# Fourteen condition blocks of the later layers formed on VectorE inside the dense feed-forward stage

## What is computed

```python
cond = jax.nn.silu(c)                                   # 1 x 1024
for i in range(2):
    mod = cond @ ada_w[i] + ada_b[i]                    # 1024 x 6144 weights for each layer
    sh1, sc1, g1, sh2, sc2, g2 = jnp.split(mod, 6)
    h = rms_norm(x, norm_mix[i]) * (1.0 + sc1) + sh1
    y = mla_mixer(h, ...) if i == 0 else gdn_mixer(h, ...)
    x = x + g1 * y
    h = rms_norm(x, norm_ffn[i]) * (1.0 + sc2) + sh2
    y = swiglu_ffn(h, ...) if i == 0 else moe_ffn(h, ...)   # dense: 1024 -> 2816 -> 1024; moe: 8 experts
    x = x + g2 * y
```

## Time and profile before

| | |
|---|---|
| median of 3 runs | 2355.04 us (2353.94 to 2355.44) |
| the profiled execution's own time | 2351.56 us |
| its span | 2349.7 us |
| TensorE matmul busy | 2132.0 us, 91% of the span |
| VectorE busy | 730.6 us, 31% |
| ScalarE busy | 429.3 us, 18% |
| mean granted TensorE clock | 0.937 of 2.4 GHz |
| HBM read | 509.11 MB, 217 GB/s over the span |

### The profile page before, as it was taken

How to read it: one execution, slowest core, us unless ns; L and a number is a source line. 1 busy time by engine, 2 the same in 40 slices (tenths; PEclk the granted TensorE clock), 3 DMA queues, 4 the chain that set the end, 5 groups by cost and what they waited for, 6 DMA issues and landing times.

```text
span 2349.7 us, 32266 instructions
## 1 busy us (share of the span) xinstructions
PE 2132.0 (91%) x13962; PEld 1463.8 (62%) x13962; DVE 730.6 (31%) x1547; ACT 429.3 (18%) x899; POOL 38.1 (2%) x34
## 2 busy tenths in 40 slices
PE   7999885478999999999899999999998899999997
PEld 4554664477754444444575688886677778648844
DVE  3484278747321111111235210004573330001001
ACT  2210324122211111111233310003222120000001
POOL 1000111000000000000000000000000000000000
PEclk9999976689989999999998999999998879999999
DMA  9643000002579999999745834308410267899695
GB/s 313 230 144 107 1 1 1 2 2 75 216 296 428 424 428 427 429 428 429 278 154 176 286 126 171 124 27 298 168 73 2 72 249 251 319 392 351 248 345 227
DMA packets 161767, 511.98 MB, mean 218 GB/s; under 512 B 8926, under 2 KB 32173, under 8 KB 148973
## 3 DMA queue, kind: packets, MB, share of 16 engines
q1 hardware_dynamic: 160816, 509.87, 56.6%
q10 hardware_dynamic: 829, 0.31, 0.1%
HBM read 509.11 MB, written 1.05 MB: 217 GB/s over the span
## 4 chain that ended last, share of the span: by engine, by line
PE 83%; DVE 9%; DMA 3%; ACT 3%; issue 2%; POOL 0%; SPq 0%; ACTq 0%; DVEq 0%; POOLq 0%
PE PS L378 34%; PE PS L2206 9%; PE PS L2227 5%; PE PS L2360 4%; PE PS L2122 4%; PE PS L2133 3%; PE PS L2058 3%; PE PS L580 3%; PE PS L2311 2%; DMA work<-in_moe_w_gate_up_dram 2%; PE PS L588 2%; PE PS L737 1%; PE PS L729 1%; DVE sq L1648 1%; DVE work L1645 1%
## 5 line engine op out<-in xcount | busy, mean ns | idle before, releaser
L378 PE MATMUL PS<-hT,work 128*128 128x256 f32 x1456 | 327.2, 386 | 2.8 <-issue 2.4
L378 PEld LDWEIGHTS PS<-hT,work 128*128 128x128 f32 x1456 | 279.0, 193 | 45.6 <-issue 5.5
L378 PE MATMUL PS<-work 128*128 128x256 f32 (+4 forms) x960 | 284.9, 457 | 2.4 <-DVE work L1803 1.5
L378 PEld LDWEIGHTS PS<-work 128*128 128x128 f32 (+2 forms) x960 | 178.0, 187 | 103.9 <-issue 76.9
L2206 PE MATMUL PS<-work,sq 128*64 128x512 f32 x1024 | 222.6, 592 | 1.3 <-ACT sq L2151 1.3
L2206 PEld LDWEIGHTS PS<-work,sq 128*64 128x64 f32 x1024 | 76.7, 137 | 143.8 <-issue 143.8
L378 PE MATMUL PS<-sq,work 128*128 128x128 f32 x1408 | 159.6, 277 | 4.9 <-DMA work<-in_moe_w_gate_up_dram 3.5
L378 PEld LDWEIGHTS PS<-sq,work 128*128 128x128 f32 x1408 | 159.3, 194 | 6.8 <-issue 6.8
L2227 PE MATMUL PS<-work 128*64 128x512 f32 x512 | 113.4, 595 | 9.9 <-issue 9.9
L2360 PE MATMUL PS<-work 128*64 128x512 f32 (+1 forms) x352 | 114.4, 593 | 1.9 <-ACT work L2390 1.9
L2188 DVE COPY work<-PS 128x1024 f32<-128x1024 f32 x22 | 26.9, 1225 | 230.2 <-PE PS L2227 117.0
(11 more groups left out here) (567 smaller groups left out, 2218.6 us busy)
## 6 DMA issues: line engine op xcount, KB each, us to landing
work<-in_ex_gate_dram SPq DMA_DIRECT2D x32, 2048.0 KB, 12.1
work<-in_ex_up_dram SPq DMA_DIRECT2D x32, 2048.0 KB, 15.2
work<-in_ex_down_dram SPq DMA_DIRECT2D x32, 2048.0 KB, 10.9
work<-in_moe_w_gate_up_dram SPq DMA_DIRECT2D x32, 2048.0 KB, 10.0
work<-in_ada_w_dram SPq DMA_DIRECT2D x24, 2048.0 KB, 9.0
work<-in_moe_w_down_dram SPq DMA_DIRECT2D x16, 2048.0 KB, 14.9
work<-in_w_ada_dram SPq DMA_DIRECT2D x12, 2048.0 KB, 8.9
work<-in_moe_w_gate_up_dram SPq DMA_DIRECT2D x16, 1536.0 KB, 13.4
```

Source lines behind the costliest of these rows:

```text
L378: ins = pe.matmul(outp, lhs, rhs, start=n == 0, stop=n == len(pairs) - 1, **kw)
```

## The change

Blocks 22 to 35 leave their places and are made in the feed-forward stage. The weights of a block are no longer multiplied on TensorE: VectorE forms the weighted sum over the eight 128-row pieces with one multiply and seven multiply-and-adds of 128x512 (`ada_sum_dve`), each waiting for the one before, and TensorE then sums over the partitions and turns the row with four one-column matmuls against ones (`ada_sum_pe`). VectorE starts a block behind tiles 1, 2, 4, 5, 6, 8, 9, 10, 12, 13, 15, 16, 17 and 19 of the 22; TensorE takes it up two tiles later, between the gate and up products. The results go to bank 7, so the tiles rotate over three banks. The 14 loads stand among the gate, up and down units of the stage, the one-turn loop around the stage is written out, and the gate and up units are used when their own tiles are complete, as before.

```diff
+    FFN_ADA = {g: n for n, g in enumerate((1, 2, 4, 5, 6, 8, 9, 10, 12, 13, 15, 16, 17, 19), N_ADA - 14)}
+    FFN_UNITS = []
+    for e in range(2):
+        for t0, n in ((0, 4), (4, 4), (8, 3)):
+            FFN_UNITS += [("gate", e, t0, n), ("up", e, t0, n)]
+            FFN_UNITS += [("ada", FFN_ADA[11 * e + t]) for t in range(t0, t0 + n) if 11 * e + t in FFN_ADA]
+        FFN_UNITS += [("down", e, t0, n) for t0, n in ((0, 4), (4, 4), (8, 3))]
...
-    for name, n in (("w_out", 2), ("ada_b", 4), ("moe1", 96), ("ada_c", 2), ("mla", 2), ("mla_q", 3), ("ada_d", 10),
-                    ("mla_out", 2), ("ada_e", 1), ("ffn", 18), ("ada_f", 1), ("gdn_kq", 4), ("ada_g", 4), ("gdn_vz", 4),
-                    ("gdn_out", 2), ("ada_h", 2), ("moe2", 72)):
+    for name, n in (("w_out", 2), ("ada_b", 4), ("moe1", 96), ("ada_c", 2), ("mla", 2), ("mla_q", 3), ("ada_d", 4),
+                    ("mla_out", 2), ("ffn", len(FFN_UNITS)), ("gdn_kq", 4), ("gdn_vz", 4), ("gdn_out", 2), ("moe2", 72)):
...
+        elif name == "ffn":
+            released_ffn(*FFN_UNITS[j])
...
+    def released_ffn(what, e, t0=0, n=0):
+
+        if what == "ada":
+            sp.wait_ge(S["ada_evac"], e + 1)
+        elif what == "down":
+            sp.wait_ge(S["weights_used"], downs_before["ffn"] + 3 * e + t0 // 4 + 1)
+        else:
+            sp.wait_ge(S["gate_up"], ex_tiles["ffn"] + 11 * e + t0 + n)
...
+    ADA_BANKS_OF.update({n: (None, 7) for n in FFN_ADA.values()})
...
+    def ada_sum_dve(n):
+
+        u = place["ada", n]
+        arrived(u, eng=dve)
+        dve.wait_ge(S["ada_cols"], n - 1)
+        w, row = unit(u, KT, 512), late_row[n % 2]
+        dv.link(dve.tensor_scalar(row, w[:, 0, :], cond[:, 0, 2:3], None, ALU.mult))
+        for k in range(1, KT):
+            ins = dve.scalar_tensor_tensor(out=row, in0=w[:, k, :], scalar=cond[:, k, 2:3], in1=row, op0=ALU.mult, op1=ALU.add)
+            if k < KT - 1:
+                dv.link(ins)
+        ins.then_inc(S["ada_evac"], 1)
...
+    def ada_sum_pe(n):
+
+        pe.wait_ge(S["params"], 1 + ada_group(n))
+        pe.wait_ge(S["ada_evac"], n + 1)
+        for m in range(4):
+            ins = pe.matmul(PS[:, ADA_BANKS_OF[n][1], m:m + 1], late_row[n % 2][:, m * P:(m + 1) * P], ones[:, 0:1],
+                            start=True, stop=True)
+        ins.then_inc(S["ada_cols"], 1)
 
...
+    def ffn_sp():
+        for j, x in enumerate(FFN_UNITS):
+            if x[0] == "ada":
+                ada_load(x[1])
+            else:
+                what, e, t0, n = x
+                load(U["ffn"] + j, ex_src("ffn", what, t0, n, e))
...
-                            if g - g0 >= 4:
-                                pe.wait_ge(S["hidden"], i * n_it + (ex_tiles[name] + g - 3))
+                            if g - g0 >= nb:
+                                pe.wait_ge(S["hidden"], i * n_it + (ex_tiles[name] + g - nb + 1))
                             for j, w in enumerate((unit(ug, KT, n * P), unit(uu, KT, n * P))):
                                 paced = 8 if name == "ffn" and g == 0 and j == 0 else None
-                                ins = product(PS[:, 4 + (g - g0) % 4, j * N:(j + 1) * N],
+                                ins = product(PS[:, 4 + (g - g0) % nb, j * N:(j + 1) * N],
                                               [(w[:, k, ptile(name, t, n)], hT[:, k, :]) for k in range(KT)], paced=paced)
                                 if j == 0 and owed:
                                     ins.then_inc(S["pair_moe1"], owed)
                                     owed = 0
                                 if j == 0 and t == 0:
                                     arrived(uu, i * rounds)
+                                if name == "ffn" and j == 0 and g - 2 in FFN_ADA:
+                                    ada_sum_pe(FFN_ADA[g - 2])
...
+                if name == "ffn" and g - 2 in FFN_ADA:
+                    ada_group_dve(FFN_ADA[g - 2])
+                if name == "ffn" and g in FFN_ADA:
+                    ada_sum_dve(FFN_ADA[g])
...
-        ada_block_pe(30)
-        ada_block_pe(31)
         pe.wait_ge(S["gd_hat"], 1)
-        pe.wait_ge(S["params"], 2 + ada_group(31))
         gd_scores_pe(2, gk)
         tiles("gdn_qb", 3, 4)
         pe.wait_ge(S["gd_read"], 2)
-        ada_block_pe(32)
-        ada_block_pe(33)
-        pe.wait_ge(S["params"], 2 + ada_group(33))
...
-        last = LAST_ADA[name]
-        ada_block_pe(last)
+        if name in LAST_ADA:
+            ada_block_pe(LAST_ADA[name])
         pe.wait_ge(S["htok"], tokens_turned[name])
         open_sums()
-        pe.wait_ge(S["params"], 2 + ada_group(last))
+        if name in LAST_ADA:
+            pe.wait_ge(S["params"], 2 + ada_group(LAST_ADA[name]))
...
-            ada_turn_pe(18 + i)
+            if i < 4:
+                ada_turn_pe(18 + i)
             if i < HP:
                 at_turn_pe(i)
             if i + 2 < HP:
                 at_scores_pe(i + 2)
             if i >= 1:
                 at_out_pe(i - 1)
-            ada_pe(19 + i)
-        ada_turn_pe(19 + HP)
+            if i < 3:
+                ada_pe(19 + i)
 
...
-            if i <= HP + 1:
+            if i < 4:
                 ada_act(18 + i)
...
-        norm_act(8, 28)
+        norm_act(8)
         ex_act("ffn")
-        norm_act(9, 29)
+        norm_act(9)
         gdn_act()
-        norm_act(10, 34)
+        norm_act(10)
...
-        ada_block_pe(28)
         ex_pe("ffn")
         norm_pe(9)
-        ada_block_pe(29)
```

More of the change, by code:

```diff
@@ L11 @@
-from contextlib import ExitStack
+from contextlib import ExitStack, nullcontext
 import math
@@ L533, in build @@
     ADA_FIRST, ADA_REST = 7, 0
-    LAST_ADA = {"moe1": 15, "moe2": 35}
-    ADA_GROUPS = [(n,) for n in range(12, 30)] + [(30, 31), (32, 33), (34,), (35,)]
-    ADA_BANKS = {"ada_b": (6, 7), "ada_c": (2, 3), "ada_d": (7, 7), "ada_e": (2, 3), "ada_f": (2, 3), "ada_g": (2, 3),
-                 "ada_h": (6, 7)}
+    LAST_ADA = {"moe1": 15}
+    ADA_GROUPS = [(n,) for n in range(12, N_ADA)]
+    ADA_BANKS = {"ada_b": (6, 7), "ada_c": (2, 3), "ada_d": (7, 7)}
     ADA_BANKS_OF = {n: ADA_BANKS[name] for name, (n0, n1) in ADA_LATER.items() for n in range(n0, n1)}
-    ADA_BANKS_OF[32] = ADA_BANKS_OF[33] = (0, 1)
+    ADA_BANKS_OF.update({n: (None, 7) for n in FFN_ADA.values()})
     def ada_group(n):
@@ L1892, in ex_unit @@
             return U[name] + [x[0:3] for x in body2].index((e, what, t0))
+        if name == "ffn":
+            return U[name] + [x[0:3] for x in FFN_UNITS].index((what, e, t0))
         per = ex_units(name)
@@ L2020, in ex_pe @@
             open_sums()
-        with pe.Fori(0, COUNT[name] // per_loop) as i:
+        nb = banks_of(name)
+        with ex_loop(pe, name) as i:
             g, owed = 0, 0
@@ L2077, in ex_bank @@
         first = [x[0] for x in ex_sequence(name)].index(ex_sequence(name)[g][0])
-        return (g - first) % 4
+        return (g - first) % banks_of(name)
     def ex_act(name):
         n_it = PER_LOOP[name] * sum(SPLIT[name])
-        with act.Fori(0, COUNT[name] // PER_LOOP[name]) as i:
+        with ex_loop(act, name) as i:
             for g in range(n_it):
@@ L2089, in ex_dve @@
         n_it = PER_LOOP[name] * sum(SPLIT[name])
[L2090 removed]
+        with ex_loop(dve, name) as i:
             for g, (turn, k, e, f) in enumerate(ex_sequence(name)):
```

42 lines of the change are left out of this document (17 added, 25 removed).

## The result

The changed kernel has a median of 2358.11 us (2352.99 to 2368.09, 20 runs) against 2353.64 us for the kernel before on the same chip (20 runs): a ratio of 1.002, 95% interval 1.0013 to 1.0027. It is slower by 4.5 us by the medians, where 3.2 us less had been forecast. Single executions far above all others (one of the kernel before at 2879.14 us, one each in experiments 7 and 9) are left out of the ratios. The profiled execution of the changed kernel took 2357.15 us (before: 2351.56).

What follows compares the result with a forecast made beforehand. TensorE was taken to bound the feed-forward stage, with room on VectorE and the queues. Terms -11.5 + 21.8 - 7.4 - 10.0 - 3.7 = -10.8 us, clock +7.6, total -3.2: 2355.0 to 2351.8 us, range 2342 to 2360.

Steps and rivals of the forecast that it cites:

- the clock's sum: Whole kernel: TensorE's clock falls in gaps the blocks had filled and behind new waits, +7.6 us in all.
- the start of the first expert: Routing: the first expert product could start 6.0 us sooner, 2.5 of them lost waiting on DMA, so -3.5 us.
- The working of the loop: Attention loop: without blocks 22 to 27 a step takes 5.7 us instead of 6.46, saving 11.5 us.
- the clock's term: Attention loop: clock falls in gaps of 2.6 us, a slow step growing by 1.1 us; +3, between 0 and 8.
- The cover: Norm 8: removing block 28 saves 0, since the first tile waits for ScalarE's hT in the norm's own chain.
- The gap's price: Norm 8: TensorE's empty gap of 4.0 us makes the clock fall once, +1.7 us.
- (c): Feed-forward stage: three condition blocks and the first down unit queue behind the third up unit; wait of 2.0 us, first half only.
- The clock behind the waits: Feed-forward stage: the two 3.6 us waits for the third up units lower the clock, +1.4 us for both.
- rival 3: Feed-forward stage: VectorE becomes the bound, 10 to some 15 us more, up to 2367 us; chance 0.05.
- rival 2: The clock falls everywhere, all gaps at their dear end, 22 us in all: +11, or 2366 us; chance 0.08.
- Rival 4: The routing gives nothing and waits (b) and (c) are a little longer: +2, 2357 us; chance 0.11.
- (b): Feed-forward stage: the third up unit of each half is issued late and waited for 3.6 us, twice: +7.2 us.

Runs made afterwards that it cites:

- experiments 7 and 9: Edits of the changed kernel: 7, six matmuls on zeros ahead of the first expert, ratio 1.0012; 9, eight blocks moved instead of fourteen, ratio 0.9947.
- e6: Changed kernel with matmuls on zeros in attention steps 4 to 6, norms 8, 9 and 10 and ahead of the first expert; ratio to the kernel before 0.9966.
- e7: Like e6, with the feed-forward stage's gate units also released after their own last product; ratio to the kernel before 0.9918, median 2336.88 us.
- e2: Changed kernel with two 128x512 matmuls on zeros in each of attention steps 4 to 8; ratio to the kernel before 1.0024.
- e3: Changed kernel with four, three and three matmuls on zeros in the gaps of norms 8, 9 and 10; ratio to the kernel before 0.9973.
- e11: Changed kernel with only four matmuls on zeros behind the sums of norm 8; ratio to the kernel before 1.0002.
- e12: Changed kernel with two matmuls on zeros in attention steps 4 and 5, one in step 6, none in 7 and 8; ratio to the kernel before 0.9998.
- e1: Changed kernel with feed-forward gate units counted as used after their own last gate product, half a tile sooner; ratio to the kernel before 0.9996.
- e10: Changed kernel with VectorE summing two of a block's eight pieces, so values differ; stage 258.5 us against 257.6, whole 2900.81 us.
- experiment 11: Eight blocks moved, norms 8 to 10 filled with matmuls on zeros, run twice, then with none and six in norm 9; ratios 0.9959, 0.9951, 0.9938, 0.9944.
- e8: Changed kernel with only six 128x496 matmuls on zeros ahead of the second mixture's first expert; ratio to the kernel before 1.0012.

## Why the prediction was wrong

The 2358.11 us lie within the range of 2342 to 2360, but the change made the kernel slower and not faster. Two of the prediction's own signs of being wrong appeared: a loop step of 7.5 us (over 6.5) and a stage of 257.6 us (over 256). The main step that failed is the clock's sum, 7.6 us, where the profile has about 16; the second is the start of the first expert, put 2.3 us too early.

*Attention.* The working of the loop held: with the clock kept, a step is 5.63 us against 5.7, and the segment is shorter by 11.1 us (61.4 against 50.3 in e6 and e7) where 11.5 were worked out. The step that failed is the clock's term, taken as +3 "between 0 and 8": it was 4.6 us (54.9 against 50.3). In it, a step at half clock was to grow by 1.1 us and grew by 1.9 (7.54 against 5.63).

*Norm 8.* The cover, ScalarE's chain, held (segment +0.1). The gap's price was 2.8 us (27.22 - 24.41), not 1.7; in the other seven profiles with this gap it was 1.5 to 3.0.

*Feed-forward stage.* Turns: 14 x 0.88 = 12.3, put at 12.6. Waits on transfers: 8.7, put at 9.2 with (c), so right in sum but not in place. The second up unit took 7.1 us to land and was waited for 3.73 us, as put (7.0 and 3.6); the first took 8.4 and was waited for 5.00. That differs between profiles: 8.2 to 8.4 us in four with this order of loads, 6.9 to 7.0 in five others, with waits of 3.5 to 3.6 (e2, e3, e6, e11, e12); why is open. (c) did not show, being covered by the longer wait; where that wait was as put, in e3, e11 and e12, it was 0.33 us and not 2.0, and in e1 3.05. The Trainium skill (DMA: Bandwidth & Descriptors, Anatomy of one DMA) would make the load 5.6 us, an estimate from a fit that the section gives for transfers issued by GpSimd. The trace has 8.4 and 7.1 us for these, which SyncE issues. The clock behind the waits: put at 1.4, measured 5.2 (0.75 + 2.70 and 0.10 + 1.69), and e1 shows that it goes with them. This is the largest single miss. Where a profile has such waits, 3.4 to 5.0 us long, it is 1.8 to 3.5 us for each.

*VectorE.* Right: 6.0 us against at most 6.3, no wait, and e10 excludes rival 3.

*Norm 9 and the delta rule.* -7.4 and -9.9: right to 0.1 us each without their clock terms (0.6 and 0.9), bound behind them included (TensorE waits 6.9 us for VectorE ahead of the triangles, which covers a slower start). The clock terms did not show up to there. The further 2.9 us from the triangles on were not foreseen and are of the kind that experiment 11 shows: the place of low-clock stretches.

*Routing.* Put were: TensorE ready at 1907.9, both loads landed near 1912.4 (its own terms, 1899.25 + 2 x 5.4 + 2.6, give 1912.65), the second needed 1.8 us behind the first product, so a start at about 1910.4. On the same scale (the ranking of the changed kernel starts 5.25 us later, 1899.51 against 1894.26) TensorE with ScalarE's 1.34 us was ready at 1907.2, the second load landed at 1912.6, and the first product started at 1912.7. So the time of both was right, and the step that failed is that the up unit would be needed only 1.8 us behind the start: the program asks for both units ahead of the first product. The first load had landed 5.6 us before it. In all fifteen profiles of the changed kernel and of its edits but e10, the product starts 0.14 us behind the second landing. The start was 2.3 us later than put. On top came 1.25 us of clock in the logits (6.99 us instead of 5.74) and 2.3 behind the wait (41.82 against 39.54 in e8), and neither had a term.

All clock losses that can be placed come to about 16 us (4.6, 2.8, 5.2, 1.3, 2.3), where the sum had 7.6 and rival 2 had 22. That rival named 16 as the point from which the change is slower by more than can be told, and this is where it came out; it was given 0.08 because every gap was said to need its dearest price, and prices in the middle, with two places that had no term, were enough. Filling the gaps of the norms alone turned the change into a gain, which makes the clock a shown cause and not an argued one. How much it takes in one execution is partly chance: the same gaps and waits cost more or less from profile to profile, and the whole of the changed kernel went from 2352.99 to 2368.09 us. Rival 4 came nearest with its 2357 us, and rightly had the routing give nothing (-0.1); but it had the rest from longer waits (b) and (c), which were 8.7 us together and not over 9.2, so its number is luck. By the rule on transposes that the prediction set against the loop (TensorE: Matmul & The Clock Gate, PE-mode transpose, of the Trainium skill), the loop without blocks would have to slow down. It did (clock 0.50, steps of 7.5 us), and stayed fast with two plain matmuls a step (1.00, 5.63 us); but the matmuls also shorten the gaps, so this does not single out the transposes.

## What to carry to other kernels

Work that sits in the gaps of a nearly saturated TensorE pays part of its own price by keeping the clock: before moving it away, count for each gap that it leaves, and for each new wait, a price behind it in the dense products. Here gaps of 3.4 to 4.0 us cost 0 to 3 us and waits of 3.4 to 5.0 us cost 1.8 to 3.5, the same length differing from profile to profile, so give a range and not one price. Move only the pieces for which TensorE was really waited (eight of fourteen here gave 0.5%), and place their loads so that no unit needed soon gets a slot released late. Look up in the program which transfers the first product behind a gap asks for, and put its start at the landing of the last of them. If a gap has to stay, useless matmuls that end inside it are cheap; outside it they cost their full time.

## What the runs showed of the hardware

A wait of 5.00 us cost TensorE 3.5 us more in the 18 us behind it; waits of 3.4 to 3.8 us cost 1.8 to 3.5, and a gap of 4.03 us 1.5 to 3.0. A part of 1600 matmul records took 193.2 and 193.1 us in two profiles with three matmuls 80 us ahead of it, and 183.2 in one with six. Two loads of 2 MB issued 0.6 us apart landed one behind the other, 7.8 and 12.7 us after their issues, with 393 GB/s once the transfers ran; with 1.5 MB each it was 7.0 and 10.6. Four one-column float32 matmuls (eight records) between dense ones cost 0.88 us. A VectorE multiply-and-add with all operands in SBUF takes as long (0.752 us for 128x512) as one with an operand in PSUM (0.751).
